# Four inverse-root chains of a decoder step: from log and exp on ScalarE to a square root on ScalarE and a reciprocal on VectorE

## The chip, the cores and the metric

The kernel runs on one core of one Trainium2 chip. The time is the device time of one execution in microseconds, and a kernel's time is the median of its runs. The engines that matter here are TensorE (PE, with its weight loads as PEld), VectorE (DVE), ScalarE (ACT), GpSimd (POOL) and the queue that issues most transfers (SP).

## The reference

One inference step of a two-layer hybrid decoder for a prompt of 256 tokens and eight samples of four new tokens each, 288 tokens in all, width 1024, in fp32. Layer 0 projects to forgetting attention (8 heads of 64) and RWKV-7 time mixing (8 heads of 64), then a dense SwiGLU; layer 1 is a causal pooling mixer, then a mixture of eight experts. Everything that the change touches is an inverse square root:

```
def rms_norm(x, g):
    y = x * lax.rsqrt(jnp.mean(x * x, axis=-1, keepdims=True) + RMS_EPS)
    return y * g

hp = modulate(xp, norm1_g[li], sh1p, sc1p)      # rms_norm, four times: before each mixer and each feed-forward
q, k = rms_norm(heads(q), q_gain), rms_norm(heads(k), k_gain)
kk = kk * lax.rsqrt(jnp.maximum(jnp.sum(kk * kk, axis=-1, keepdims=True), 1e-24))
y = (y - mean) * lax.rsqrt(var + GN_EPS) * ln_w + ln_b                # group norm of the RWKV heads
```

## The kernel before

Activations lie transposed: 128 channels on the partitions, the 288 tokens along the free axis, so that the model's width is 8 such slices. One program is written out by hand for each engine, and the engines meet at counted semaphores; no scheduler reorders anything. On each engine the order is the order of the code. An engine's operation that follows another through memory waits for a semaphore of it, so that nearly every VectorE operation starts after the one before has ended.

TensorE's results go into eight PSUM banks, handed out in turn by `banks.open`: the ninth opening takes the bank of the first, and TensorE waits there until the reader of that bank has given its semaphore. Weights stream from HBM into a ring of six slots of 2 MB.

Seven inverse roots are taken. ScalarE's helper `inverse_root` (L1756) takes a logarithm in place and then an exponential of -0.5 times it. The sums under the roots come from a matmul with ones, which repeats a sum on all partitions that need it, so that the roots are taken on full tiles:

- `root(0)` to `root(3)`, called from the program of ScalarE, on `rstd`, 128 x 288. VectorE's `mean_of(i)` (L1997) writes the mean into `rstd`, waits for `rooted` and multiplies `hT = xT * rstd`; the next matmuls read `hT`.
- the norms of q and k (`qk_rooted`) on the whole `tmpT`, 128 x 2304, in the middle of the input projection. VectorE multiplies them into q and k in its section for `i == 5`, between its copies of the projection's results out of the banks.
- the norm of the RWKV key (`kk_rooted`) on 128 x 1152. VectorE then multiplies `kkT` and after it reads the three banks `bon0` to `bon2`. TensorE opens after `bon2` the banks `kt40`, `kt41`, `ss3`, `kt50`, `kt51`, and the next one, `ss4`, takes the bank of `bon0`. The names `kt` and `ss` are the transposed past keys and the scores of a sample.
- the group norm (`gn_rooted`) on 128 x 1152. After it VectorE finishes the mixer's result `yT` (L2264 to L2270), and the output projection starts.

The compiled program has an ACT_TABLE_LOAD on ScalarE wherever the compiler switches tables: before every `Ln` and every `Exp` of an inverse root, and before none of the copies and squares.

Of the kernel before, what the change touches and what calls it, by code (L numbers as in the profile page):

```python
# [21 lines left out]
ACT = mybir.ActivationFunctionType  # L22
# [7 lines left out]
N = NP + NS  # L30
# [3 lines left out]
HC = HW // P  # L34
# [257 lines left out]
def spread(ap, axis, n):  # L292

    ap = ap.unsqueeze(axis)
    shape = list(ap.shape)
    shape[axis] = n
    return ap.to_broadcast(shape)


def flat(t):  # L300
    return t[:, :, :].rearrange("p a b -> p (a b)")
# [42 lines left out]
def build_program(nc, a, y_p, y_s, k_p, k_s, v_p, v_s, lf_p, lf_s, st_p, st_s, sh_p, sh_s, pool_p, pool_s):  # L344

    ctx = ExitStack()
    with ctx:
        def sb(name, shape, dt=F32):
            return ctx.enter_context(nc.sbuf_tensor(name, shape, dt))

        s = Named(nc, ctx)
        once = Once(s)

        def sums(name, which, n):

            return s(f"sums_{which}"), 3 * ("kks", "bon", "gnm", "gnv").index(name) + n
# [10 lines left out]
        def K(name, rows=P):  # L367
            at, n = CONST[name]
            return const[0:rows, at:at + n]

        ident = K("ident")
        xT = sb("xT", [P, DC, N])
        hT = sb("hT", [P, DC, N])
        tmpT = sb("tmpT", [P, DC, N])
# [5 lines left out]
        rstd = sb("rstd", [P, N])  # L380
# [116 lines left out]
            return t.rearrange("p (c a) k -> p c a k", a=2)[:, :, a, :]  # L497

        small = sb("small", [P, 64])

        plan = sb("plan", [1, NE + 2 * MORE + 1], I32)
        mix_stores = [0]
# [1229 lines left out]
        def _(act):  # L1732
            me = Counted(act)
            chain = s("act_chain")

            def copy(out, in_, sem):
                me.give(act.activation(out, in_, ACT.Copy), sem)  # L1737
# [15 lines left out]
                        act.wait_ge(s("res"), DC * (i - 1) + c + 1)  # L1753
                    me.give(act.activation(tmpT[:, c, :], xT[:, c, :], ACT.Square), s("squared"))

            def inverse_root(v, sem):  # L1756

                me.step(act.activation(v, v, ACT.Ln), chain)
                me.give(act.activation(v, v, ACT.Exp, scale=-0.5), sem)

            def root(i):
                act.wait_ge(s("ms_read"), i + 1)
                inverse_root(rstd[:, :], s("rooted"))

            square_all(0)
            root(0)

            def ada(layer, i):
                k = 12 * layer + i
                act.wait_ge(s("ada_mm"), k + 1)  # L1770
                if k >= 2:
                    act.wait_ge(s("folded"), k - 1)
                copy(adap[layer][:, k % 2, :], banks[f"ada{layer}_{i}"][:, :], s("ada_copied"))
# [4 lines left out]
            def proj_chunk(n):  # L1778
                kind, idx, _, m = WCHUNKS[n]
                dst = {"f": fqkv, "r": rp}[kind]  # L1780
                return dst[0:m, idx, :], banks[f"win{n}"][0:m, 0:N]
# [3 lines left out]
            for i, (_, _, cs) in enumerate(WIN):  # L1785
                for _ in cs:
                    if n % 2:
                        act.wait_ge(s("win_mm"), n + 1)
                        copy(*proj_chunk(n), s("win_act"))
                    n += 1  # L1790
                if i == 2:
                    act.wait_ge(s("win_dve"), HC)
                    act.wait_ge(s("win_act"), HC)
                    me.give(act.activation(flat(tmpT), fqkv[:, 0:2 * HC, :].rearrange("p a b -> p (a b)"), ACT.Square),
                            once.give("qk_squared"))
                ada(0, 4 + i)
                if i == 4:
                    act.wait_ge(s("qkms_read"), 6)
                    inverse_root(flat(tmpT), once.give("qk_rooted"))
            act.wait_ge(*once("lf_abs"))  # L1800
            me.step(act.activation(lftmp[:, 0, :], lftmp[:, 0, :], ACT.Exp), once.give("lf_exp"))
            act.wait_ge(*once("lf_one"))
# [45 lines left out]
            def scores_of(q):  # L1848
                act.wait_ge(s("ss_mm"), q + 1)
                copy(psm[32 * (q % 4):32 * (q % 4) + 32, q // 4, :], banks[f"ss{q}"][0:32, 0:PAST + NT], s("ss_copied"))  # L1850

            for q in range(NB):
                for half in range(2):
                    act.wait_ge(s("kt_mm"), 2 * q + half + 1)
                    if q >= 2:
                        act.wait_ge(s("ss_mm"), q - 1)
                    copy(ktb[:, q % 2, 2 * half:2 * half + 2, 0:PAST],
                         banks[f"kt{q}{half}"][:, :].rearrange("p (c k) -> p c k", c=2), s("kt_copied"))
                copy(ktb[:, q % 2, :, PAST:PAST + NT], fqkv[:, HC:2 * HC, NP + NT * q:NP + NT * (q + 1)], s("kt_copied"))
                if q:  # L1860
                    scores_of(q - 1)
                if q == 2:
                    act.wait_ge(*sums("kks", "read", 3))
                    inverse_root(flat(tmpT)[:, 0:HC * N], once.give("kk_rooted"))
            scores_of(NB - 1)
            act.wait_ge(*once("cum_ready"))
            me.give(act.activation(lw[:, :, NP:N], lw[:, :, NP:N], ACT.Exp), s("decay_exp"))
# [48 lines left out]
            copy(yT[:, HC:2 * HC, NP:N], banks["syt"][:, 0:HC * NS].rearrange("p (c t) -> p c t", c=HC), once.give("syt_copied"))  # L1916
            act.wait_ge(*once("gn_centred"))
            me.give(act.activation(flat(tmpT)[:, 0:HC * N], flat(yT)[:, HC * N:2 * HC * N], ACT.Square), once.give("gn_squared"))
            act.wait_ge(*sums("gnv", "read", 3))
            inverse_root(flat(tmpT)[:, 0:HC * N], once.give("gn_rooted"))  # L1920


            square_all(1)
# [41 lines left out]
        def _(dve):  # L1965
            me = Counted(dve)
            chain = s("dve_chain")
            TT, TS, STT = dve.tensor_tensor, dve.tensor_scalar, dve.scalar_tensor_tensor

            def do(ins, sem=None):  # L1970
                me.step(ins, sem or chain)
# [8 lines left out]
            def mod_tile(layer, i):  # L1980

                dve.wait_ge(s("folded"), 12 * layer + i + 1)
                bias = vT[:, 0, 48 * layer + 4 * i:48 * layer + 4 * i + 4]
                do(TT(modT[layer][:, 4 * i:4 * i + 4, :], banks[f"fold{layer}_{i}"][:, 0:36].rearrange("p (j m) -> p j m", j=4),
                      spread(bias, 2, 9), ALU.add), s("mod_ready"))
# [11 lines left out]
            def mean_of(i):  # L1997
                dve.wait_ge(s("ms_ready"), i + 1)
                do(TS(rstd[:, :], banks[f"ms{i}"][:, 0:N], 1.0 / D, RMS_EPS, ALU.mult, ALU.add), s("ms_read"))
                dve.wait_ge(s("rooted"), i + 1)  # L2000
                do(TT(hT[:, :, :], xT[:, :, :], spread(rstd[:, :], 1, DC), ALU.mult))  # L2001

            def by_seq(ap):
# [32 lines left out]
            for i, (_, _, cs) in enumerate(WIN):  # L2036
                for kind, idx, _, m in cs:
                    if n % 2 == 0:
                        dve.wait_ge(s("win_mm"), n + 1)
                        src = banks[f"win{n}"][0:m, 0:N]  # L2040
                        if kind == "l":
                            do(TS(rstd[0:H, :], src, fbias[:, 0:1], None, ALU.add), s("win_dve"))
                        else:
                            do(dve.tensor_copy({"f": fqkv, "r": rp}[kind][0:m, idx, :], src), s("win_dve"))
                    n += 1
                if i == 2:
                    dve.wait_ge(*once("vec2_turned"))
                    do(dve.tensor_copy(vT[:, 1:3, :], banks["vec2"][:, 0:2 * P].rearrange("p (i f) -> p i f", i=2)),
                       once.give("vec2_copied"))
                    qg = vT[:, 1, VB_QG:VB_QG + 1]  # L2050
                    do(TS(qg, qg, DH ** -0.5, None, ALU.mult))
                if i == 4:

                    for k in range(6):
                        dve.wait_ge(s("qkms"), k + 1)
                        do(TS(flat(tmpT)[:, 384 * k:384 * (k + 1)], banks[f"qkms{k}"][:, 0:384], 1.0 / DH, RMS_EPS, ALU.mult, ALU.add),
                           s("qkms_read"))
                if i == 5:
                    dve.wait_ge(*once("qk_rooted"))
                    dve.wait_ge(s("win_act"), HC)  # L2060
                    for part, g, sem in ((1, VB_KG, "k_ready"), (0, VB_QG, "q_ready")):
                        v = fqkv[:, HC * part:HC * (part + 1), :].rearrange("p a b -> p (a b)")
                        r = flat(tmpT)[:, HC * N * part:HC * N * (part + 1)]
                        do(STT(v, v, vT[:, 1, g:g + 1], r, ALU.mult, ALU.mult), once.give(sem))
                if i:
                    mod_tile(0, 3 + i)
# [52 lines left out]
            def fl(t):  # L2119
                return t.rearrange("p a b -> p (a b)")  # L2120
# [16 lines left out]
                do(TS(flat(tmpT)[:, 384 * i:384 * (i + 1)], banks[f"kks{i}"][:, 0:384], 1e-24, None, ALU.max), s("sums_read"))  # L2137
            dve.wait_ge(*once("kk_rooted"))
            r = flat(tmpT)[:, 0:HC * N]
            do(STT(fl(kkT), fl(kkT), -1.0, r, ALU.mult, ALU.mult))  # L2140

            for i in range(3):
# [118 lines left out]
                   s("sums_read"))  # L2261
            dve.wait_ge(*once("gn_rooted"))
            r = flat(tmpT)[:, 0:HC * N]
            do(TT(y2, y2, r, ALU.mult))  # L2264
            for c in range(HC):
                v = yT[:, HC + c, :]
# [355 lines left out]
```

## Time and profile before

| | |
|---|---|
| median of 3 runs | 1998.54 us (1998.26 to 2000.01) |
| the profiled execution | 2002.73 us, of which the span of the trace is 2000.9 us |
| PE busy | 1812.9 us (91% of the span), 9750 instructions |
| DVE busy | 413.6 us (21%), 772 instructions |
| ACT busy | 225.0 us (11%), 452 instructions |
| POOL busy | 185.2 us (9%), 198 instructions |
| mean granted TensorE clock | 0.917 of full speed |

The shares are averages over stages of different kinds. From about 940 us on the program is the experts, a long run of matmuls; before that, dependent steps of several engines alternate with runs of matmuls. All seven inverse roots lie before 913 us. Times in the rows are microseconds from the start of the span, unless a column says nanoseconds.

### The profile page before, as it was taken

What the parts mean: (1) busy time and instruction counts of PE and PEld (TensorE: products, weight loads), DVE (VectorE), ACT (ScalarE), POOL (GpSimd) and SP (SyncE); (2) the same over time, 40 slices, a digit from 0 to 9 for tenths busy, and PEclk for the clock granted to TensorE, in tenths of its full rate; (3) what the DMA queues carried; (4) which work ended last, traced back from release to release, by engine and by line L of the source; (5) the groups of instructions that cost most, each with busy time, mean ns of one, the idle gap of its engine ahead of it and who ended that gap; (6) DMA issues with size and microseconds to landing.
All of it is one profiled execution on the core that took longest, in us unless ns stands there. A gap on an engine that the chain in (4) does not pass through costs nothing.

```text
span 2000.9 us, 22754 instructions
## 1 busy us (share of the span) xinstructions
PE 1812.9 (91%) x9750; PEld 1166.1 (58%) x9751; DVE 413.6 (21%) x772; ACT 225.0 (11%) x452; POOL 185.2 (9%) x198
## 2 busy tenths in 40 slices
PE   6999687575789999967999999999999999999998
PEld 4766344465467777745555555666555555566664
DVE  2012643857220111174100000001000000010002
ACT  2022142110110000022100000000000000000001
POOL 4002701835000000021000000000000000000000
PEclk8999587656689999977999999999999999999999
DMA  9761031100364554840899999965999999889991
GB/s 346 268 231 64 25 112 31 43 1 4 142 217 158 196 195 167 300 183 11 303 369 339 361 334 347 339 247 199 357 362 364 363 361 367 300 305 383 378 389 64
DMA packets 216499, 476.59 MB, mean 238 GB/s; under 512 B 15823, under 2 KB 24403, under 8 KB 215971
## 3 DMA queue, kind: packets, MB, share of 16 engines
q1 hardware_dynamic: 212971, 471.94, 64.5%
q0 software_dynamic: 3232, 3.08, 0.5%
q8 instruction: 80, 1.31, 0.3%
q14 instruction: 24, 0.20, 0.0%
q10 hardware_dynamic: 192, 0.07, 0.0%
HBM read 470.79 MB, written 4.62 MB: 238 GB/s over the span
## 4 chain that ended last, share of the span: by engine, by line
PE 84%; DVE 5%; POOL 3%; SPq 2%; ACT 2%; DMA 2%; issue 2%; DVEq 0%; POOLq 0%; ACTq 0%
PE bank L1261 82%; POOL ring L2455 2%; DMA ring<-in_ada_w 1%; POOL other L2464 1%; PE bank L749 1%; ACT ring L1737 1%; DVE xT L2017 1%; SPq L2564 1%; SPq L2529 0%; DVE ring L2109 0%; DVE ring L2100 0%; DVE hT L2001 0%; SPq L2555 0%; PE bank L1394 0%; DVE yT L2326 0%
## 5 line engine op out<-in xcount | busy, mean ns | idle before, releaser
L1261 PE MATMUL bank<-other,ring 128*128 128x192 f32 (+4 forms) x3360 | 491.3, 314 | 51.7 <-POOL ring L2455 29.3
L1261 PEld LDWEIGHTS bank<-other,ring 128*128 128x128 f32 (+1 forms) x3360 | 454.2, 193 | 108.9 <-issue 58.8
L1261 PE MATMUL bank<-ring,tmpT 128*64 128x512 f32 (+2 forms) x1120 | 340.1, 604 | 0.0
L1261 PE MATMUL bank<-hT,ring 128*128 128x288 f32 (+2 forms) x1472 | 306.7, 384 | 9.3 <-DVE hT L2013 9.3
L1261 PEld LDWEIGHTS bank<-hT,ring 128*128 128x128 f32 (+2 forms) x1472 | 234.6, 191 | 80.4 <-issue 18.8
L1261 PE MATMUL bank<-ring,other 128*64 128x512 f32 x1120 | 247.8, 595 | 0.6 <-issue 0.6
L1261 PEld LDWEIGHTS bank<-ring,tmpT 128*64 128x64 f32 (+2 forms) x1120 | 106.1, 149 | 204.1 <-issue 202.2
L1261 PEld LDWEIGHTS bank<-ring,other 128*64 128x64 f32 x1120 | 78.2, 137 | 147.7 <-issue 146.6
L1015 DVE TENSOR_TENSOR other<-other,bank 64x512 f32<-64x512 f32 x35 | 23.8, 679 | 641.7 <-ACT other L883 641.7
L1261 PE MATMUL bank<-ring 128*64 128x64 f32 (+6 forms) x468 | 78.9, 413 | 13.5 <-ACT ring L1737 8.8
L1261 PE MATMUL bank<-hT,other 128*128 128x288 f32 (+4 forms) x304 | 69.3, 420 | 6.6 <-DVE hT L993 5.8
L1261 PEld LDWEIGHTS bank<-ring 128*64 128x64 f32 (+4 forms) x468 | 48.0, 204 | 40.3 <-ACT ring L1737 13.4
L2455 POOL TENSOR_TENSOR ring<-ring,const 64x256 f32<-64x256 f32 x48 | 63.7, 1326 | 54.8 <-DVE ring L2217 46.6
L1737 ACT ACTIVATE ring<-bank 128x512 f32<-128x512 f32 (+8 forms) x110 | 44.9, 437 | 175.6 <-PE bank L1261 114.3
L1261 PEld LDWEIGHTS bank<-hT,other 128*128 128x128 f32 (+2 forms) x304 | 46.2, 193 | 29.8 <-issue 19.8
L877 ACT ACTIVATE other<-bank 128x384 f32<-128x384 f32 (+2 forms) x42 | 18.3, 437 | 379.0 <-PE bank L1261 379.0
L1009 DVE TENSOR_TENSOR tmpT<-other,bank 128x384 f32<-128x384 f32 (+2 forms) x42 | 20.5, 488 | 186.7 <-PE bank L1261 144.7
L883 ACT ACTIVATE other<-bank 64x512 f32<-64x512 f32 x35 | 20.8, 593 | 337.6 <-PE bank L1261 337.6
L1261 PE MATMUL bank<-ring,silucT 128*32 128x512 f32 x384 | 46.6, 616 | 4.9 <-DMA ring<-in_ada_w 4.9
L2287 DVE TENSOR_TENSOR other<-other,bank 128x288 f32<-128x288 f32 x22 | 10.0, 454 | 163.5 <-PE bank L1261 163.5
L1737 ACT ACTIVATE other<-bank 128x512 f32<-128x512 f32 (+4 forms) x44 | 22.4, 518 | 177.7 <-PE bank L1261 143.8
L1261 PE MATMUL bank<-yT,other 128*128 128x288 f32 x80 | 26.0, 492 | 16.1 <-DVE yT L2270 10.5
(310 smaller groups left out, 1052.3 us busy)
## 6 DMA issues: line engine op xcount, KB each, us to landing
ring<-in_moe_w_gate SPq DMA_DIRECT2D x56, 2048.0 KB, 10.2
ring<-in_moe_w_up SPq DMA_DIRECT2D x56, 2048.0 KB, 11.1
ring<-in_moe_w_down SPq DMA_DIRECT2D x56, 2048.0 KB, 9.6
ring<-in_ada_w SPq DMA_DIRECT2D x24, 2048.0 KB, 13.7
ring<-in_w_in SPq DMA_DIRECT2D x5, 2048.0 KB, 12.6
ring<-in_ffn_w_gate SPq DMA_DIRECT2D x5, 2048.0 KB, 10.2
ring<-in_ffn_w_up SPq DMA_DIRECT2D x5, 2048.0 KB, 9.1
ring<-in_ffn_w_down SPq DMA_DIRECT2D x5, 2048.0 KB, 17.4
```

The source lines that it names most:

```text
L749: last = pe.transpose(B[TURN][:, HALF * j:HALF * (j + 1)], ea[:, P * j:P * (j + 1)], ident[0:HALF, 0:HALF])
L877: act.activation(sgw[:, 2 * half:2 * half + 2, 0:n], by_half(B[X + half], n), ACT.Silu).then_inc(s("w_silu"), 1)
L883: act.activation(sg, B[GU][HALF:P, :], ACT.Silu).then_inc(s("l_silu"), 1)
L1009: dve.tensor_tensor(actw[:, w % 2, j, 0:n], sgw[:, j, 0:n], by_half(B[X + half], n), ALU.mult).then_inc(s("w_act"), 1)
L1015: dve.tensor_tensor(ea, sg, B[GU][0:HALF, :], ALU.mult).then_inc(s("l_act"), 1)
L1261: return pe.matmul(out, lhsT, rhs, start=start, stop=stop, skip_group_check=True)
L1737: me.give(act.activation(out, in_, ACT.Copy), sem)
L2017: do(STT(xT[:, j, 0:NP], src[:, 0:NP], gate_[:, j, 0:1], xT[:, j, 0:NP], ALU.mult, ALU.add))
L2287: do(TT(ffact[:, i % 2, n % 4, :], ffsilu[:, n % 2, :], banks[f"up{n}"][:, 0:N], ALU.mult), s("act_ready"))
L2455: me.step(pool.tensor_tensor(nm[o, n % 2], of(gt[o, n % 2], a_)[:, :, 0:L], mask, ALU.mult), s("nm_ready") if a_ else s("pool_chain"))
L2464: me.step(pool.tensor_tensor(vk, spread(sval[:, t, :], 2, DH), spread(svec[:, t, 3, :], 1, 32), ALU.mult), s("vk_ready"))
L2564: sp.dma_start(svec[2 * H * q + f:2 * H * (q + 1):2].rearrange("p t i k -> p (t i) k"), scratch[q].rearrange("t i h k -> h (t i) k")).then ...
```

## The change

The seven uses of `inverse_root` become `root_of`, one square root on ScalarE, and VectorE takes a reciprocal in place right after its wait for the root. `root(i)` and the group norm get `early_root`, a square root of one element into an unused cell, ahead of the wait. The norms of q and k and of the RWKV key get no early root.

```
+        root_of_one = small[0:1, 61:62]
...
-            def inverse_root(v, sem):
-                me.step(act.activation(v, v, ACT.Ln), chain)
-                me.give(act.activation(v, v, ACT.Exp, scale=-0.5), sem)
+            def early_root():
+                act.activation(root_of_one, K("ident")[0:1, 0:1], ACT.Sqrt)
+            def root_of(v, sem):
+                me.give(act.activation(v, v, ACT.Sqrt), sem)
             def root(i):
+                early_root()
                 act.wait_ge(s("ms_read"), i + 1)
-                inverse_root(rstd[:, :], s("rooted"))
+                root_of(rstd[:, :], s("rooted"))
...
-                    inverse_root(flat(tmpT), once.give("qk_rooted"))
+                    root_of(flat(tmpT), once.give("qk_rooted"))
...
-                    inverse_root(flat(tmpT)[:, 0:HC * N], once.give("kk_rooted"))
+                    root_of(flat(tmpT)[:, 0:HC * N], once.give("kk_rooted"))
...
+            early_root()
             act.wait_ge(*sums("gnv", "read", 3))
-            inverse_root(flat(tmpT)[:, 0:HC * N], once.give("gn_rooted"))
+            root_of(flat(tmpT)[:, 0:HC * N], once.give("gn_rooted"))
...
                 dve.wait_ge(s("rooted"), i + 1)
+                do(dve.reciprocal(rstd[:, :], rstd[:, :]))
                 do(TT(hT[:, :, :], xT[:, :, :], spread(rstd[:, :], 1, DC), ALU.mult))
...
                     dve.wait_ge(*once("qk_rooted"))
+                    do(dve.reciprocal(flat(tmpT), flat(tmpT)))
...
             dve.wait_ge(*once("kk_rooted"))
             r = flat(tmpT)[:, 0:HC * N]
+            do(dve.reciprocal(r, r))
             do(STT(fl(kkT), fl(kkT), -1.0, r, ALU.mult, ALU.mult))
...
             dve.wait_ge(*once("gn_rooted"))
             r = flat(tmpT)[:, 0:HC * N]
+            do(dve.reciprocal(r, r))
             do(TT(y2, y2, r, ALU.mult))
```

On ScalarE the compiled program has 20 table loads before and 13 after. At the group norm and `root(1)`, ScalarE's order before:

```order
L1918 ACTIVATE tmpT<-yT 128x1152 [waits vector_once]
L1758 ACT_TABLE_LOAD
L1758 ACTIVATE tmpT<-tmpT 128x1152 [waits sums_read]
L1759 ACT_TABLE_LOAD
L1759 ACTIVATE tmpT<-tmpT 128x1152 [waits act_chain]
L1754 ACTIVATE tmpT<-xT 128x288 [waits res] x8
L1758 ACT_TABLE_LOAD
L1758 ACTIVATE rstd<-rstd 128x288 [waits ms_read]
L1759 ACT_TABLE_LOAD
```

and the same place of the changed kernel:

```order
L1922 ACTIVATE tmpT<-yT 128x1152 [waits vector_once]
L1759 ACT_TABLE_LOAD
L1759 ACTIVATE small<-const 1x1
L1762 ACTIVATE tmpT<-tmpT 128x1152 [waits sums_read]
L1755 ACTIVATE tmpT<-xT 128x288 [waits res] x8
L1759 ACTIVATE small<-const 1x1
L1762 ACTIVATE rstd<-rstd 128x288 [waits ms_read]
```

In both, a load stands ahead of the waiting activation and carries no wait itself. The load and the second activation behind the wait are gone.

Later than the RWKV key's root ScalarE takes exponentials of the cumulated decay. Its order there before (`ss_mm` rows are the copies of the scores, `vector_once` is VectorE's `cum_ready` and then `psm_shifted`):

```order
L1737 ACTIVATE ring<-bank 32x260 [waits ss_mm] x2
L1867 ACTIVATE other<-other 128x4x32 [waits vector_once]
L1868 ACTIVATE tmpT<-tmpT 128x1024
L1869 ACTIVATE tmpT<-tmpT 128x1024
L1870 ACTIVATE hT<-hT 128x1024
```

and after:

```order
L1738 ACTIVATE ring<-bank 32x260 [waits ss_mm] x2
L1871 ACT_TABLE_LOAD
L1871 ACTIVATE other<-other 128x4x32 [waits vector_once]
L1872 ACTIVATE tmpT<-tmpT 128x1024
L1873 ACTIVATE tmpT<-tmpT 128x1024
L1874 ACTIVATE hT<-hT 128x1024
```

A table load has come in behind the copies. The same holds, not shown, for the first exponential of the forget gate (L1801) and for that of the router (L1955).

VectorE's order at the RWKV key, before:

```order
L2137 TENSOR_SCALAR tmpT<-bank 128x384 [waits sums_mm,sums_read] x2
L2140 SCALAR_TENSOR_TENSOR yT<-yT,tmpT 128x1152 [waits scalar_once,sums_read]
L2145 TENSOR_TENSOR other<-bank,other 128x384 [waits sums_mm,dve_chain]
L2145 TENSOR_TENSOR other<-bank,other 128x384 [waits sums_mm,sums_read] x2
L2147 TENSOR_SCALAR other<-other 128x1152 [waits sums_read]
```

and after:

```order
L2144 TENSOR_SCALAR tmpT<-bank 128x384 [waits sums_mm,sums_read] x2
L2147 RECIPROCAL tmpT<-tmpT 128x1152 [waits scalar_once,sums_read]
L2148 SCALAR_TENSOR_TENSOR yT<-yT,tmpT 128x1152 [waits dve_chain]
L2153 TENSOR_TENSOR other<-bank,other 128x384 [waits sums_mm,dve_chain]
L2153 TENSOR_TENSOR other<-bank,other 128x384 [waits sums_mm,sums_read] x2
L2155 TENSOR_SCALAR other<-other 128x1152 [waits sums_read]
```

The reciprocal has come in between the wait for ScalarE (`scalar_once`) and the multiplication; the reads of the `bon` banks stand behind both. The other six reciprocals stand at the same kind of place.

## Rows read from the trace of the kernel before

**Rows 1.** The page's chain that ended last: shares of the span by engine.
```profile
PE 84%; DVE 5%; POOL 3%; SPq 2%; ACT 2%; DMA 2%; issue 2%; DVEq 0%; POOLq 0%; ACTq 0%
```

**Rows 2.** ScalarE's groups by form: busy us, mean ns | idle before.
```profile
L1758 ACT ACT_TABLE_LOAD x7 | 9.0, 1283 | 0.1
L1759 ACT ACT_TABLE_LOAD x7 | 9.0, 1283 | 0.1
```

**Rows 3.** VectorE's groups by form, same columns.
```profile
L2001 DVE TENSOR_TENSOR hT<-xT,rstd 128x2304 f32<-128x2304 f32 x4 | 10.2, 2559 | 9.3 <-ACT rstd L1759 9.3
...
L2264 DVE TENSOR_TENSOR yT<-yT,tmpT 128x1152 f32<-128x1152 f32 x1 | 1.4, 1359 | 3.8 <-ACT tmpT L1759 3.8
...
L2108 DVE RECIPROCAL small<-small 128x2 f32<-128x2 f32 x8 | 1.3, 166 | 0.3
...
L2362 DVE RECIPROCAL other<-other 128x3 f32<-128x3 f32 x1 | 0.2, 178 | 0.0
...
L2363 DVE TENSOR_TENSOR other<-other 128x3 f32<-128x3 f32 x1 | 0.2, 166 | 0.0
```

**Rows 4.** Timeline at root(1): start, us, engine, line, operation [idle before].
```profile
570.94 0.46 DVE L1999 TENSOR_SCALAR rstd<-bank 128x288 f32<-128x288 f32 x1 [2.95 <-PE bank L1261]
571.43 0.44 ACT L1758 ACTIVATE rstd<-rstd 128x288 f32<-128x288 f32 x1 [1.66 <-DVE rstd L1999]
571.89 1.28 ACT L1759 ACT_TABLE_LOAD   x1
...
573.73 2.56 DVE L2001 TENSOR_TENSOR hT<-xT,rstd 128x2304 f32<-128x2304 f32 x1 [2.33 <-ACT rstd L1759]
```

**Rows 5.** Timeline at the group norm, to the output projection.
```profile
522.88 1.16 ACT L1758 ACTIVATE tmpT<-tmpT 128x1152 f32<-128x1152 f32 x1 [3.27 <-DVE tmpT L2260]
524.06 1.28 ACT L1759 ACT_TABLE_LOAD   x1
...
526.62 1.36 DVE L2264 TENSOR_TENSOR yT<-yT,tmpT 128x1152 f32<-128x1152 f32 x1 [3.77 <-ACT tmpT L1759]
...
532.68 14.87 PE L1261 MATMUL bank<-yT,other 128*128 128x288 f32 x48 [10.51 <-DVE yT L2270]
```

**Rows 6.** Timeline in the input projection, around VectorE's multiplications of q and k.
```profile
147.06 0.46 DVE L2044 COPY other<-bank 128x288 f32<-128x288 f32 x1 [7.30 <-PE bank L1261]
147.56 2.87 DVE L2064 SCALAR_TENSOR_TENSOR other<-other,vT,tmpT 128x1152 f32<-128x1152 f32 x2
...
167.90 0.51 PE L1261 MATMUL bank<-hT,ring 128*128 128x288 f32 x1
```

**Rows 7.** Timelines of ScalarE, VectorE and TensorE at the RWKV key.
```profile
286.51 1.16 ACT L1758 ACTIVATE tmpT<-tmpT 128x1152 f32<-128x1152 f32 x1
...
290.26 1.36 DVE L2140 SCALAR_TENSOR_TENSOR yT<-yT,tmpT 128x1152 f32<-128x1152 f32 x1 [16.11 <-ACT tmpT L1759]
...
291.65 1.74 DVE L2145 TENSOR_TENSOR other<-bank,other 128x384 f32<-128x384 f32 x3
...
296.07 1.94 PE L1261 MATMUL bank<-ring 128*32 128x260 f32 x8
...
299.84 1.09 PE L1447 MATMUL bank<-const,ring 128*128 128x128 f32 x8 [0.79 <-DMA ring<-in_cache_fox_logf]
```

**Rows 8.** Timeline at the exponentials of the decay.
```profile
311.30 0.31 ACT L1867 ACTIVATE other<-other 128x128 f32<-128x128 f32 x1
...
315.08 0.69 DVE L2158 TENSOR_REDUCE small<-ring 128x2 f32<-128x520 f32 x1 [2.07 <-ACT ring L1872]
```

**Rows 9.** Timeline of VectorE behind root(0), and at the forget gate and router.
```profile
40.74 0.20 DVE L1984 TENSOR_TENSOR modT<-bank,vT 128x36 f32<-128x36 f32 x1 [9.60 <-PE bank L1261]
...
186.28 0.44 ACT L1801 ACTIVATE ring<-ring 8x288 f32<-8x288 f32 x1 [2.83 <-DVE ring L2075]
...
930.83 0.17 DVE L2369 COPY small<-bank 128x8 f32<-128x8 f32 x1 [2.15 <-PE bank L1261]
```

**Rows 10.** Stretch of the windows view: us, PE busy, granted clock, DMA share, GB/s.
```profile
532.60:535.00 2.40, 2.32 (x5) 0.50 0.24 59
```

## The prediction

> **What bounds the kernel now.** I read the chain that ended last first, then the groups by form of ScalarE and VectorE, then the timelines at the seven roots. The chain is 84% TensorE; VectorE has 5% of it and ScalarE 2% [rows 1]. So nearly nothing of this change touches the bound by its busy time; what counts is where TensorE stands still because a root is not there yet. At root(1) the reader sees such a place: VectorE writes the mean, ScalarE takes the logarithm, loads a table for 1.28 us and takes the exponential, and VectorE sat idle 2.33 us before it multiplies [rows 4]. The four such waits sum to 9.3 us [rows 3]. The group norm is the same with longer tiles: VectorE waits 3.77 us, and TensorE starts the output projection right after VectorE's last step, after 10.51 us of idleness [rows 5]. The table loads are 14 of 1283 ns [rows 2], but the seven ahead of a logarithm are not on the path: at the group norm ScalarE sat idle 3.27 us between its load and the logarithm [rows 5]. Transfers have 2% of the chain [rows 1], and those of weights in it lie ahead of 45 us; nothing behind these places is there to take up a delay, so a microsecond at one of them is a microsecond of the kernel.
>
> **What is removed.** Per root, behind the wait, one table load and one activation. For root(1) to root(3) the square root should last what the logarithm does, 0.44 us, and would end where the load now starts; the removed part is 1.28 + 0.44 = 1.72 us and small gaps [rows 4]. At the group norm it is 1.28 + 1.16 = 2.44 us [rows 5]. The early root of one element and its load run in ScalarE's idle time, where the load of the logarithm ran: cost nothing while the 3.27 us (and 1.66 us at root(1)) of idleness behind it cover the 0.2 us that a short activation takes [rows 4, 5]. Without that cover it would be 0.2 us each.
>
> **What is added: the reciprocal.** Its price at 288, 1152 and 2304 elements decides everything, and the trace has it only for 2 and 3 elements. An ordinary two-operand pass costs 1359 ns for 1152 elements and 2559 ns for 2304, so 1.04 ns for each further element and about 160 ns for one element [rows 3]. The reciprocal of 2 elements takes 166 ns: its second element costs 6 ns. That of 3 takes 178 ns, in a tile where an ordinary pass over 3 elements takes 166 ns, so about 164 ns for one, and the two others cost 7 ns each. Taking the two reciprocals against one another, the third element costs 12 ns [rows 3]. The lower bound is the ordinary 1.04 ns, the upper one 12 ns. These are differences of single clock steps and of different tiles, but none of the readings that use a reciprocal lies near 1 ns. I take 7 ns, from the comparison within one tile: 153 + 7N ns, that is 2.17 us for 288, 8.22 us for 1152, 16.28 us for 2304.
>
> The Trainium skill speaks against the change here: "VectorE: DVE Perf Modes", section "Walkthrough: the 8-slice pipeline in each mode", says that a reciprocal runs iterative divide operations with a repeat count of 8. Read as 8 cycles of that page's 0.96 GHz clock for each element, an estimate of 8.33 ns, it would make the sum below about 16 us in place of 9.5.
>
> **The sum, place by place.**
> - root(0): VectorE next waits, 9.60 us long, for the modulation at 40.74 us [rows 9]. The reciprocal's 2.2 us against 1.7 us saved vanish there: 0. With less cover it would be +0.4.
> - norms of q and k: ScalarE is long done when VectorE comes to them. The reciprocal goes in after the copy that ends at 147.52 us, ends at 163.8, and the two multiplications (2.87 us) at 166.7, the next read of a bank (0.20 us, the same operation as in [rows 9]) at 167.0. Late next is TensorE's opening at 167.90, the ninth after the bank that this read frees [rows 6]. 0.9 us are left: 0. Beyond 7.4 ns an element TensorE would stand there, 2.3 us for each further ns.
> - RWKV key: the square root ends at 286.51 + 1.16 = 287.67 us. The reciprocal runs from 287.77 to 295.99, the multiplication (1.36) to 297.4, and the first read of a `bon` bank (a third of 1.74) to 298.0 [rows 7]. TensorE wants that bank for `ss4` at 296.07: it waits 1.95 us. Of these 0.79 us would have been idle before the next transposes at 299.84 [rows 7]: +1.2. At 6.0 ns an element this term ends.
> - decay exponentials: before, ScalarE starts them at 311.30 at once behind the last copy, the table of exponentials being loaded. Now the load stands there. VectorE waits for the end of this run with 2.07 us of idleness, so all of the load is on the path: +1.28, by the 1283 ns of the other loads [rows 2, 8].
> - group norm: the square root ends at 522.88 + 1.16 = 524.04, the reciprocal at 524.14 + 8.22 = 532.36, and VectorE multiplies at 532.4 where it was 526.62: +5.8 [rows 5].
> - root(1) to root(3): square root to 571.87, reciprocal from 571.97 to 574.14, multiplication at 574.17, before 573.73: +0.44, three times +1.3 [rows 4].
> - forget gate: the new load falls in 2.83 us of idleness ahead of that exponential; 0. Router: the load delays VectorE's six small steps by about 1.3 us, but VectorE waits 2.15 us for TensorE behind them; 0 [rows 9]. Without that cover each would cost 1.28.
>
> Together 0 + 0 + 1.2 + 1.28 + 5.8 + 1.3 = **9.6 us slower**. Against its own profiled execution of 2002.73 us that is 2012.3; that one is 4.2 us above the median of the runs, 1998.54, and the difference is put on the median: **2008.1 us**.
>
> A second rule of the skill concerns the loads. Rows first: at root(1) the load starts at 571.89; 1.28 us of load and 0.44 us of exponential end at 573.61, and VectorE multiplies at 573.73 [rows 4]. "ScalarE: Activation LUTs", section "What ACT_TABLE_LOAD costs", adds a drain of about 1.38 us to each. By it the load added at the decay would cost 2.66 us and the sum be 1.4 us larger; there is no room for a drain in these rows, and I stay with 1.28.
>
> **The rivals.**
> - *The reciprocal is an ordinary pass* at 1.04 ns an element: 0.46, 1.36 us. For it speaks only that all other passes here are; against it the 12 ns between the two sizes. Then root(1) to root(3) gain 1.27 us each, the group norm 1.1 us, the key nothing, and the load still costs 1.28: -3.6 us, **1994.9**. This is the case on the other side. It turns at about 2.9 ns an element, where the gains of the four waits just pay the load; if two elements went per cycle it would be 1.2 us lower still.
> - *Between*, 3 to 5 ns an element, if the small reciprocals carry a fixed part that I have put on the elements: at 4.5 ns the group norm is +2.9, the three roots -0.8, the load +1.28: **2001.9**.
> - *The steep reading*, 12 ns: 3.6, 14.0 and 27.8 us. The projection then loses 10.5, the key 6.9, the group norm 11.5, the three roots 5.6, the load 1.28: +35.8, **2034**. For it speaks the pair of reciprocals; against it that they lie in different tiles, with strides of their own.
> - *TensorE's clock*: after the group norm's 10.51 us of idleness the granted clock is 0.50 of full, 1.2 of 2.4 GHz [rows 5, 10]. A longer wait can't lower it there. The new wait at `ss4` could cost a fall where there was none, some microseconds more; I give it no case of its own but it lies in the range.
>
> **How the numbers follow.** 6 to 9 ns an element has a chance of 0.70 and gives 2005 to 2018, worked as above at 6 and at 9; the ordinary pass 0.12, the cases between 0.08, the steep one 0.10. I leave out the ordinary pass and most of the steep side: 2001 to 2019. A measurement of this kernel tells about 0.2%, 4 us, from no change, its runs lying 1.8 us apart. The ordinary pass at -3.6 is just within it, faster by more only with two elements per cycle: faster 0.05. Within 0.2%: the rest of that case and most of the cases between, 0.14. Slower 0.81.
>
> **What would show it.** The reciprocals' durations at 288, 1152 and 2304 elements, on which all hangs: 2.2, 8.2 and 16.3 us. VectorE's idleness before the reciprocals at 0.6 us for root(1) to root(3) and about 1.3 us at the group norm; the output projection 5.8 us further from the group norm's sums than before. TensorE waiting for a bank at `ss4`, about 2 us, and not at all in the input projection. A load of 1.28 us between the last score copy and the decay's first exponential. Thirteen table loads. I am wrong if the reciprocals take about 1.4 us at 1152 elements (then all stalls shrink), if TensorE stands in the projection, or if the clock falls at `ss4`.

## The result and the profile after

| | before | after |
|---|---|---|
| median of 6 runs each, us | 1999.23 (1997.69 to 2000.6) | 2006.2 (2005.28 to 2008.2) |
| ratio, 95% interval | | 1.0037 (1.0024 to 1.0049) |
| profiled execution, us (span) | 2002.73 (2000.9) | 2007.59 (2005.7) |
| granted clock, mean | 0.917 | 0.92 |

The changed kernel is 7.0 us slower by the medians (4.8 to 9.8 by the interval); 9.6 us were forecast. The page of the profile of the changed kernel, called after from here on, says:

```profile
span 2005.7 us, 22753 instructions
PE 1811.2 (90%) x9750; PEld 1164.4 (58%) x9751; DVE 451.1 (22%) x779; ACT 210.6 (11%) x443; POOL 185.5 (9%) x198
PE 83%; DVE 6%; POOL 3%; SPq 2%; issue 2%; ACT 2%; DMA 1%; ACTq 0%; DVEq 0%; POOLq 0%
```

TensorE still holds the chain [rows 1]; VectorE has gone from 5% to 6% of it. The prediction hung on the reciprocal's price. VectorE's groups by form, after (busy us, mean ns | idle before):

```profile
L2066 DVE RECIPROCAL tmpT<-tmpT 128x2304 f32<-128x2304 f32 x1 | 14.6, 14553 | 0.0
L2006 DVE RECIPROCAL rstd<-rstd 128x288 f32<-128x288 f32 x4 | 7.8, 1953 | 2.3 <-ACT rstd L1762 2.3
L2272 DVE RECIPROCAL tmpT<-tmpT 128x1152 f32<-128x1152 f32 x1 | 7.4, 7353 | 1.3 <-ACT tmpT L1762 1.3
```

From 1152 to 2304 elements it takes 14553 - 7353 = 7200 ns more, 6.25 ns an element; from 288 to 1152, 5400 ns, 6.25 again. The constant is 7353 - 1152 x 6.25 = 153 ns, the very one of the forecast, and 153 + 2 x 6.25 = 166 ns is the small reciprocal of [rows 3]. The idle time before the four of 288 elements is 2.3 us, against 9.3 before the multiplications of [rows 3]: the waits for ScalarE shrank as meant, and VectorE's own work took their place.

Timeline of after at root(1) and at the group norm (start, us, engine, line, operation, idle before), which answer to [rows 4] and [rows 5]:

```profile
576.56 0.46 DVE L2004 TENSOR_SCALAR rstd<-bank 128x288 f32<-128x288 f32 x1 [2.95 <-PE bank L1262]
577.05 0.44 ACT L1762 ACTIVATE rstd<-rstd 128x288 f32<-128x288 f32 x1 [2.87 <-DVE rstd L2004]
577.59 1.95 DVE L2006 RECIPROCAL rstd<-rstd 128x288 f32<-128x288 f32 x1 [0.58 <-ACT rstd L1762]
579.58 2.56 DVE L2007 TENSOR_TENSOR hT<-xT,rstd 128x2304 f32<-128x2304 f32 x1
```

```profile
524.36 1.16 ACT L1762 ACTIVATE tmpT<-tmpT 128x1152 f32<-128x1152 f32 x1 [2.98 <-DVE tmpT L2268]
525.62 7.35 DVE L2272 RECIPROCAL tmpT<-tmpT 128x1152 f32<-128x1152 f32 x1 [1.30 <-ACT tmpT L1762]
533.01 1.36 DVE L2273 TENSOR_TENSOR yT<-yT,tmpT 128x1152 f32<-128x1152 f32 x1
...
539.07 6.10 PE L1262 MATMUL bank<-yT,other 128*128 128x288 f32 x15 [15.41 <-DVE yT L2279]
```

From the mean (VectorE's 0.46 us) to the multiplication are 3.02 us at root(1), 2.79 before: +0.23. At the group norm, from the square root's start to the multiplication 8.65 us, before 3.74: +4.91, and TensorE stands 15.41 us where it stood 10.51.

ScalarE at the decay exponentials, after, answers to [rows 8]:

```profile
311.33 0.38 ACT L1738 ACTIVATE ring<-bank 32x260 f32<-32x260 f32 x1 [2.52 <-PE bank L1262]
311.72 1.28 ACT L1871 ACT_TABLE_LOAD   x1
313.02 0.31 ACT L1871 ACTIVATE other<-other 128x128 f32<-128x128 f32 x1
...
316.79 0.69 DVE L2166 TENSOR_REDUCE small<-ring 128x2 f32<-128x520 f32 x1 [3.35 <-ACT ring L1876]
```

The new load stands behind the last copy, and VectorE's wait is 3.35 us where it was 2.07: 1.28 us more, the whole load. The first exponential follows 0.02 us behind the load's end. "ScalarE: Activation LUTs" of the Trainium skill, section "What ACT_TABLE_LOAD costs", adds about 1.38 us of drain to each load; these rows have no place for it.

TensorE and VectorE at the RWKV key and `ss4`, after, answer to [rows 7]:

```profile
288.13 7.35 DVE L2147 RECIPROCAL tmpT<-tmpT 128x1152 f32<-128x1152 f32 x1 [15.61 <-ACT tmpT L1762]
...
297.61 1.91 PE L1262 MATMUL bank<-ring 128*32 128x260 f32 x8 [1.62 <-DVE other L2153]
...
300.49 1.09 PE L1448 MATMUL bank<-const,ring 128*128 128x128 f32 x8
```

The forecast wait at `ss4` is there, 1.62 us long, and the transposes behind it at 300.49 wait for nothing, where they had stood 0.79 us for a transfer.

In the input projection (answering to [rows 6]) nothing waits:

```profile
145.91 14.55 DVE L2066 RECIPROCAL tmpT<-tmpT 128x2304 f32<-128x2304 f32 x1
...
163.41 0.20 DVE L1989 TENSOR_TENSOR modT<-bank,vT 128x36 f32<-128x36 f32 x1
...
166.25 10.07 PE L1262 MATMUL bank<-hT,ring 128*128 128x288 f32 x39
```

The read that frees the bank ends at 163.61, and TensorE opens there at 166.25 without a wait. The place is free because of these 2.64 us of cover. ScalarE has thirteen table loads in place of twenty.

### The profile page after: what moved, and what is told of

Read it like the earlier page. It is cut to its first block, busy times and chain, and to the rows that moved or that the text cites. A ratio compares the mean times of both kernels' runs of the same rounds, so it can differ in the third digit from the quotient of the medians.

```text
span 2005.7 us, 22753 instructions
## 1 busy us (share of the span) xinstructions
PE 1811.2 (90%) x9750; PEld 1164.4 (58%) x9751; DVE 451.1 (22%) x779; ACT 210.6 (11%) x443; POOL 185.5 (9%) x198
## 4 chain that ended last, share of the span: by engine, by line
PE 83%; DVE 6%; POOL 3%; SPq 2%; issue 2%; ACT 2%; DMA 1%; ACTq 0%; DVEq 0%; POOLq 0%
PE bank L1262 81%; POOL ring L2464 2%; POOL other L2473 1%; SPq L2538 1%; PE bank L750 1%; SPq L2548 1%; ACT ring L1738 1%; DVE xT L2023 1%; DMA ring<-in_w_in 1%; SPq L2573 1%; DVE ring L2116 0%; DVE ring L2107 0%; DVE hT L2007 0%; DVE tmpT L2272 0%; DVE tmpT L2147 0%
## 6 DMA issues: line engine op xcount, KB each, us to landing
ring<-in_ada_w SPq DMA_DIRECT2D x24, 2048.0 KB, 13.5
```

## The experiments

e4 and e8 start from the kernel before, the others from the changed one. Whole times of one and the same kernel spread by 8 to 9 us between runs (before beside e1 to e4: 1998.8, 1994.68 to 2002.55 in 19 runs; beside e5 to e8: 2000.81, 1994.45 to 2003.73 in 12), so most verdicts are read from the place in the trace that the edit touches. Each kernel has one trace, of one execution. `inverse_root` below is the function of before.

**e1: the table of exponentials loaded early at the decay.**

```diff
                     root_of(flat(tmpT)[:, 0:HC * N], once.give("kk_rooted"))
+                    act.preload_act_table(ACT.Exp)
```

> The changed kernel, with the table of exponentials loaded right behind the RWKV key's square root, where ScalarE has idle time, instead of behind the last score copy. Theory (the load is on the path there): the decay's exponentials start at once behind the copy, 1.28 us earlier, and the time falls by about 1.3 us, to 1.0030 of before (some 2005). Rival (VectorE's own steps end last there): no change, 1.0037.

Measured: 2005.18 us (2004.71 to 2007.23, 5 runs), ratio 1.0035 (1.0021 to 1.0048). ScalarE and VectorE of e1:

```profile
286.42 1.28 ACT L1869 ACT_TABLE_LOAD   x1
...
313.91 0.70 DVE L2167 TENSOR_REDUCE small<-ring 128x2 f32<-128x520 f32 x1 [2.07 <-ACT ring L1877]
```

The load lies in the scores, and VectorE's wait is 2.07 us again, as before the change. So the load's 1.28 us were on the path and this line takes them back; the whole time, 1.0 us below after, agrees but could not have shown it. From the key's squares on ScalarE to that reduction e1 needs 45.28 us and before 45.08. With the load gone, 0.20 us are left for the key's reciprocal; e6 below shows how little that says.

**e2: the group norm with logarithm and exponential again.**

```diff
-            early_root()
             act.wait_ge(*sums("gnv", "read", 3))
-            root_of(flat(tmpT)[:, 0:HC * N], once.give("gn_rooted"))
+            inverse_root(flat(tmpT)[:, 0:HC * N], once.give("gn_rooted"))
...
-            do(dve.reciprocal(r, r))
```

> The changed kernel with the group norm alone taken back to log and exp, no reciprocal there. Theory (7.35 us of reciprocal against 2.44 us of load and exponential, all of it on the path): 4.9 us faster than the changed kernel, 1.0012 of before (some 2001.5). Rival (the change's cost sits in its loads and in TensorE's clock, the reciprocal being partly made up for later): less than half of that, 1.0025 or more.

Measured: 2003.79 us (1998.74 to 2007.27, 10 runs), ratio 1.0025 (1.0014 to 1.0035). The rows of e2:

```profile
520.89 1.16 ACT L1762 ACTIVATE tmpT<-tmpT 128x1152 f32<-128x1152 f32 x1 [3.66 <-DVE tmpT L2271]
...
524.63 1.36 DVE L2275 TENSOR_TENSOR yT<-yT,tmpT 128x1152 f32<-128x1152 f32 x1 [3.77 <-ACT tmpT L1763]
...
530.70 14.07 PE L1262 MATMUL bank<-yT,other 128*128 128x288 f32 x48 [10.50 <-DVE yT L2281]
```

Activation to multiplication is 3.74 us, as in [rows 5], and TensorE's idle time is 10.50 us: the place gives back 4.91 us. The whole time did not come down by as much: 2.4 us by the medians, short of the 4.9 us expected, and from its ratio of 1.0025 alone the rival could not be told apart. The ten runs are 8.5 us apart. The trace settles more: from the group norm's squares to VectorE's mean at root(1), with the output projection in between, e2 takes 53.38 us, after 57.86 and e1 58.23. (Before, which runs e2's steps there, takes 53.79.) So the 4.5 to 4.9 us are still saved at root(1), and up to there the reciprocal is not made up for. Why the median of the whole times shows only half of it stays open; the last section has a candidate. e3 pulls the same lever harder.

**e3: the group norm's reciprocal three times** (the second undoes the first, so the values stand).

```diff
             do(dve.reciprocal(r, r))
+            do(dve.reciprocal(r, r))
+            do(dve.reciprocal(r, r))
```

> The changed kernel with three reciprocals in a row at the group norm in place of one (two of them undo one another). Theory: twice 7.35 us and 0.04 us of gap each on the path, 14.8 us slower than the changed kernel, 1.0111 of before (some 2021). Rival (part of a stall there is given back, TensorE's clock returning earlier behind it): 1.0105 or less, 12 to 13.5 us; with the clock unmoved the runs of matmuls behind it last the same.

Measured: 2022.37 us (2020.2 to 2026.42, 4 runs), ratio 1.0125 (1.011 to 1.0141), 16.2 us above after. The rows of e3:

```profile
522.44 7.35 DVE L2272 RECIPROCAL tmpT<-tmpT 128x1152 f32<-128x1152 f32 x1 [1.30 <-ACT tmpT L1762]
...
537.21 7.35 DVE L2274 RECIPROCAL tmpT<-tmpT 128x1152 f32<-128x1152 f32 x1
544.60 1.36 DVE L2275 TENSOR_TENSOR yT<-yT,tmpT 128x1152 f32<-128x1152 f32 x1
```

From the square root's start to the multiplication are 23.43 us, for 8.65 in after: 14.78 us more, two reciprocals with their gaps. TensorE stands 30.19 us before the output projection, 14.78 more than in after, and from the squares to the mean at root(1) e3 takes 73.45 us, 15.6 more. So the trace shows nothing given back up to root(1), against the rival's 12 to 13.5 us. The 16.2 us of the whole time agree, but the intervals of the two ratios are too wide to exclude the rival by themselves.

**e4: logarithm and exponential from one table set, loaded ahead of the waits.** It starts from before. At root(0), the key and root(2) the set that has both functions is loaded by name.

```diff
             def root(i):
+                if i in (0, 2):
+                    act.preload_act_table_set("natural_log_exp_and_others")
...
+                    act.preload_act_table_set("natural_log_exp_and_others")
                     act.wait_ge(*sums("kks", "read", 3))
```

> The kernel before, with log and exp everywhere, but the one table set that serves both loaded ahead of the waits of root(0), the RWKV key and root(2). Theory (a load between log and exp costs its 1.28 us where the wait is on the path): gone from the forget gate, the group norm and root(1) to root(3), five times 1.28, while tanh needs a load of its own that comes onto the path, so 5 us faster than before, 0.9974 (some 1994). Rival (the set's own tables cost more, or TensorE's clock takes the gain back): 0.9985 to 1.000.

Measured: 1992.96 us (1991.22 to 1998.1, 10 runs), ratio 0.9974 (0.9965 to 0.9984): faster than both kernels, and the 0.9974 that was expected. The rows of e4 at the group norm, and VectorE's at root(1):

```profile
519.34 1.16 ACT L1758 ACTIVATE tmpT<-tmpT 128x1152 f32<-128x1152 f32 x1 [4.50 <-DVE tmpT L2263]
520.54 1.16 ACT L1759 ACTIVATE tmpT<-tmpT 128x1152 f32<-128x1152 f32 x1
521.80 1.36 DVE L2267 TENSOR_TENSOR yT<-yT,tmpT 128x1152 f32<-128x1152 f32 x1 [2.49 <-ACT tmpT L1759]
...
566.55 2.56 DVE L2004 TENSOR_TENSOR hT<-xT,rstd 128x2304 f32<-128x2304 f32 x1 [1.05 <-ACT rstd L1759]
```

At the group norm no load stands between the two activations. VectorE waits 2.49 us in place of 3.77, and 1.05 in place of 2.33: 1.28 us at each of these places and also at root(2) and root(3), and nothing is handed to VectorE. At the forget gate VectorE's step that waits for the second function starts 2.80 us after the gains are taken, in place of 4.07, so 1.27 us earlier. The groups of this trace have 8 loads, before had 20. "ScalarE: Activation LUTs" of the Trainium skill, section "Table sets: the hidden batching unit", says that a logarithm and then an exponential need one load, as a joint set has both. Here that holds in e4, where the set is asked for by name, and not in before, where each activation got a load of its own [rows 2].

One load moved onto the path instead, the one ahead of the tanh, which before had found its table in place. Timeline of e4:

```profile
256.05 0.28 ACT L1737 ACTIVATE yT<-bank 128x128 f32<-128x128 f32 x1 [1.24 <-PE bank L1261]
256.34 1.28 ACT L1837 ACT_TABLE_LOAD   x1
257.64 0.44 ACT L1837 ACTIVATE other<-other 64x288 f32<-64x288 f32 x1
```

TensorE waits 2.14 us there in place of 0.71, so this costs 1.43 us. The local gains are then 4 x 1.28 + 1.27 - 1.43 = 5.0 us, and the ratio says 5.2.

**e5: two more reciprocals of 1152 elements at q and k** (again they undo each other), added to after; one run.

```diff
                     do(dve.reciprocal(flat(tmpT), flat(tmpT)))
+                    do(dve.reciprocal(flat(tmpT)[:, 0:HC * N], flat(tmpT)[:, 0:HC * N]))
+                    do(dve.reciprocal(flat(tmpT)[:, 0:HC * N], flat(tmpT)[:, 0:HC * N]))
```

> The changed kernel with two more reciprocals of 1152 elements (they undo one another) behind the one of q and k. In the changed kernel VectorE's next reads of banks end 2.6 us before TensorE wants the first of them. Theory (nine openings of cover): TensorE waits 14.8 - 2.6 = 12 us there, and the forget gate's steps come 12 us later after their start. Rival (no cover, or cover of more banks): 14.8 us, or under 8.

Measured: 2019.84 us, 13.6 above after's median. VectorE and TensorE of e5:

```profile
169.55 7.35 DVE L2068 RECIPROCAL tmpT<-tmpT 128x1152 f32<-128x1152 f32 x1
...
179.84 0.20 DVE L1989 TENSOR_TENSOR modT<-bank,vT 128x36 f32<-128x36 f32 x1
...
180.19 13.99 PE L1262 MATMUL bank<-hT,ring 128*128 128x288 f32 x48 [12.21 <-DVE modT L1989]
```

TensorE stands 12.21 us, as the theory had it (12), and the row names VectorE's read of a modulation bank, the chain of steps that the forecast gave. Of 14.77 us added, 2.56 were covered, close to the 2.64 read off after's rows. The place was free by its slack, not because VectorE is out of TensorE's way.

**e6: the key with logarithm and exponential again**; one run.

```diff
-                    root_of(flat(tmpT)[:, 0:HC * N], once.give("kk_rooted"))
+                    inverse_root(flat(tmpT)[:, 0:HC * N], once.give("kk_rooted"))
...
-            do(dve.reciprocal(r, r))
```

> The changed kernel with the RWKV key's norm alone taken back to log and exp. Theory: TensorE's wait of 1.6 us for a bank there goes, worth some tenths because transfers of pages end there as well, and the decay's load goes, 1.28 us, since the key's exponential leaves its table: 1.4 to 1.9 us from the square of the key to VectorE's sum over the sample scores. Rival (the load moves elsewhere onto the path): less than 0.6 us.

Measured: 2002.9 us. From the key's squares to the reduction are 44.75 us. Against e2 and e3 (46.5 us), which run after's steps there, that is 1.8 us less, within the 1.4 to 1.9 expected. Against e1 (45.28), which like e6 has no load on the path, it is 0.5 us less, where e1 beside before gave 0.2. But before and e6 run the same instructions on this stretch and are themselves 0.33 us apart, so the key's reciprocal is shown to cost some tenths at most, and its size is not told closer. `ss4` waits for no bank here; TensorE stands 0.24 and 0.62 us for transfers instead, the second of them here:

```profile
303.86 1.09 PE L1448 MATMUL bank<-const,ring 128*128 128x128 f32 x8 [0.62 <-DMA ring<-in_cache_fox_logf]
```

**e7: root(0) to root(3) with logarithm and exponential again**; one run.

```diff
-                early_root()
                 act.wait_ge(s("ms_read"), i + 1)
-                root_of(rstd[:, :], s("rooted"))
+                inverse_root(rstd[:, :], s("rooted"))
...
-                do(dve.reciprocal(rstd[:, :], rstd[:, :]))
```

> The changed kernel with root(0) to root(3) alone taken back to log and exp. Theory: from VectorE's mean to its multiplication 2.79 us as in the kernel before, instead of 3.02, so 0.23 us less at each of root(1) to root(3), 0.7 us in all; the time by itself can't tell that. If TensorE's phase of clock makes the 1.2 us by which the router's matmuls came later in the changed kernel, it can stand here or not, whatever the router's load; if the load makes it, it stays only where a load stands there, and here none does, since root(3) leaves the table of exponentials.

Measured: 2008.24 us, too near to after for one run to say more. In the trace of e7 at root(1):

```profile
577.01 0.46 DVE L2007 TENSOR_SCALAR rstd<-bank 128x288 f32<-128x288 f32 x1 [2.95 <-PE bank L1262]
...
579.80 2.56 DVE L2009 TENSOR_TENSOR hT<-xT,rstd 128x2304 f32<-128x2304 f32 x1 [2.33 <-ACT rstd L1763]
```

That is 2.79 us, as before: the 0.23 us of each of the three are the square root and reciprocal in place of load and exponential, and nothing else. From the mean of root(1) to the multiplication of root(3) after takes 341.81 us, e7 341.24 and before 341.61; the 0.7 us that three times 0.23 make can't be told closer than that. What e7 says of the router stands with the router below.

**e8: e4 with the tanh's table loaded among the score exponentials.**

```diff
                 if k < 7:
                     exponentials(k + 1)
+                if k == 6:
+                    act.preload_act_table_set("sigmoid_and_others")
```

> The kernel before with the one table set for log and exp, as tried already, and the sigmoid's set, which has tanh too, loaded behind the last exponential of the prompt's attention, so that neither tanh nor sigmoid finds a load ahead of it. Theory: tanh starts 1.28 us earlier behind its wait, of which some is paid back by ScalarE's copies in the attention, 0.5 to 1.3 us faster than that kernel, 0.9970 of before (some 1993). Rival (the copies behind the load are just as much on the path): 0.9974, the same.

Measured: 1989.49 us (1985.04 to 1995.4, 7 runs), ratio 0.9946 (0.9926 to 0.9965), the fastest version here. Timeline of e8:

```profile
249.63 1.28 ACT L1828 ACT_TABLE_LOAD   x1
...
254.97 0.28 ACT L1737 ACTIVATE yT<-bank 128x128 f32<-128x128 f32 x1 [1.24 <-PE bank L1261]
255.14 0.43 ACT L1839 ACTIVATE other<-other 64x288 f32<-64x288 f32 x1
```

The tanh starts 0.17 us after the copy's start, in e4 1.59 us after it: 1.42 us nearer. That is what the edit is shown to do. From that copy to the key's squares e8 takes 13.18 us and e4 13.95, so of the 1.42 us only 0.8 are left there in these two traces. The step from e4's 0.9974 to 0.9946 is 0.0028, or 5.6 us by the ratios and 3.5 us by the medians, and the intervals meet at 0.9965. Both were measured beside different runs of before, and 0.9970 was expected. The part beyond 1.4 us is not accounted for, and that e8 is faster than e4 is likely but not shown by the times alone.

## Why the prediction was nearly right

Slower was forecast and is what came, by the mechanism that the sum gave. What differs is one number, the 7 ns an element, which is 6.25. It came from the reciprocal of 3 elements, whose 178 ns [rows 3] lie 6 ns above the 153 + 3 x 6.25 = 172 ns of the line; the other reading of the same rows, 6 ns for the second element, was the nearer one. "VectorE: DVE Perf Modes" of the Trainium skill, section "Walkthrough: the 8-slice pipeline in each mode", speaks of a repeat count of 8; read as 8 cycles an element it was the estimate of 8.33 ns, and the rows show less.

| place | forecast, us | measured, us | read from |
|---|---|---|---|
| root(0) | 0 | 0 | VectorE waits 5.70 and 6.91 us for TensorE behind it |
| forget gate | 0 | 0 | VectorE's steps 4.08 for 4.07 |
| norms of q and k | 0 | 0 | no wait; e5: 2.6 us of cover |
| RWKV key | +1.2 | +0.2 to +0.5 | e1 with before, e1 with e6; before and e6, alike there, differ by 0.3 |
| decay exponentials | +1.28 | +1.28 | wait 3.35 for 2.07; e1 |
| group norm | +5.8 | +4.9 | 8.65 for 3.74; e2, e3 |
| root(1) to root(3) | 3 x 0.44 | 3 x 0.23 | 3.02 for 2.79; e7 |
| router | 0 | 0 | see below |
| sum | 9.6 | 7.1 to 7.4 | whole times: 7.0 |

That the sum and the whole times meet within 0.4 us is partly luck: the interval of the ratio, 4.8 to 9.8 us, holds the forecast's 9.6 as well as the 7.1 to 7.4, and only the rows decide between them.

**The mis-sized term is the reciprocal's price**: 8.22 us at 1152 elements was 7.35, and 2.17 at 288 was 1.95. The 0.9 us at the group norm and 0.2 at each of three roots are this alone.

**The key** was forecast at +1.2 us, from a wait of 1.95 less 0.79 of transfer waits. With 7.35 us, the same steps give 287.77 + 7.35 = 295.12, the multiplication to 296.5, the first bank read to 297.1, and a wait of 1.0 us at `ss4`; e1 has 1.17 and e3 0.97. The transfer waits that it swallows are 0.79 and, two steps on, 0.15 us, so 0.94. What is left is 0.1 to 0.2, in keeping with the few tenths measured. By these rows a slightly dearer reciprocal would have counted in full, and a cheaper one not at all. The wait is 1.33 us in e2 and 1.62 in e7 and after; the last two are those in which the clock had fallen just ahead (below).

**The rivals.** The ordinary pass (1.36 us at 1152 elements) and the steep reading (14 us) are both excluded by 7.35 us, and the case between at 4.5 ns by the same row. (The further gain at two elements per cycle is 1.05 us by the forecast's own terms, 0.52 ns on 3 x 288 + 1152 elements, and not 1.2.) The fall of the clock at `ss4` did not come: the granted clock stays at 1.00 from 290 to 310 us in after, e1, e2, e3, e6 and e7.

**The router.** There after is 1.2 us later than before between root(3)'s multiplication and the rank copy (19.46 us for 18.28), where the forecast had 0 for the load. The five other traces that have the load there stand thus: e1, e2, e5 and e6 need 19.5 us, e3 17.89. The three others without it need 17.9 (e4 and e8) and 18.1 us (e7). e7's expectation named this: the 1.2 us would be gone there if the load made them, and they are, so e7 does not clear the load. e3 does, by its rows beside those of after. VectorE's rank copies are

```profile
937.83 0.17 DVE L2378 COPY small<-bank 128x8 f32<-128x8 f32 x1 [2.06 <-PE bank L1262]
```

in after and

```profile
948.37 0.17 DVE L2380 COPY small<-bank 128x8 f32<-128x8 f32 x1 [0.51 <-PE bank L1262]
```

in e3. Counted from root(3)'s multiplication, the load starts at 14.5 us in both and VectorE's last small step behind it at 17.2 us in both. What differs is TensorE: in the 3 us from the load's start on, its granted clock is 1.00 in e3 and 0.50 in after, so that at the load's start it had come back in the one and not in the other. The load comes too late to have kept it from coming back. The load itself has 0.5 us of cover in e3 and 2.1 in after. The windows of after, in front of the rank copy and behind it (us, PE busy (x), PEld, DVE, ACT and POOL busy (x), granted clock, DMA share, GB/s):

```profile
930.00:936.00 6.00, 6.00 (x35) 5.47 (x34) 3.46 (x23) 4.27 (x8) 0.00 (x0) 0.50 0.00 0
946.00:950.00 4.00, 4.00 (x15) 2.77 (x15) 0.49 (x1) 0.44 (x1) 0.00 (x0) 0.96 0.00 0
```

and the same places of before:

```profile
927.00:931.00 4.00, 3.73 (x32) 3.46 (x30) 1.60 (x9) 2.31 (x6) 0.00 (x0) 0.90 0.00 0
939.00:943.00 4.00, 4.00 (x11) 2.62 (x11) 0.49 (x1) 0.44 (x1) 0.00 (x0) 0.69 0.00 0
```

In after the granted clock is at 0.50 (1.2 of 2.4 GHz) ahead of the ranks and back at 0.96 in the gather; in before it is the other way about. From root(3)'s multiplication to the end of the span the six traces with the load take 1087.4 to 1087.9 us and the four without it 1087.9 to 1088.4: what is lost ahead of the ranks comes back behind them, and the load costs nothing there, as forecast. Why five of the six traces with the load have the late return of the clock and none of the four without it stays open.

## What to carry to other kernels

Price a replacement by the size of its tile and not by its count: a reciprocal at 6.25 ns an element on a VectorE that TensorE waits for beats a table load of 1.28 us and an activation only in small tiles. An estimate of the break-even from root(1)'s and the group norm's rows (+0.23 us at 288 elements, +4.91 at 1152, so 5.4 ns an element) is near 250 elements. When a table load is on the path, ask first whether one set holds both functions and load it by name ahead of the wait; that gave the 1.28 us back at each wait and put nothing elsewhere, as long as the next function with another table (here the tanh) gets its load in idle time too. Before believing a whole time, look at the place: the 0.23 us at each root repeats to 0.01 us in the traces, where whole times differed by 8. But a longer stretch of one trace carries the clock's own differences, and two kernels that are alike on it show how large they are.

## What the runs showed that was not expected

**The same program, another clock.** TensorE's granted clock does not change at the same instruction in each execution. After and e1 run the same program up to the key. Windows of TensorE alone in after, over the transposes and scores at 278 to 286 us (us, PE busy, granted clock, DMA share, GB/s):

```profile
278.00:282.00 4.00, 2.53 (x12) 0.84 0.83 240
282.00:286.00 4.00, 4.00 (x19) 0.74 0.87 253
```

and of e1:

```profile
278.00:282.00 4.00, 2.47 (x15) 1.00 0.88 254
282.00:286.00 4.00, 3.60 (x22) 1.00 0.81 248
```

Eight matmuls of the scores took 3.50 us at the fallen clock in after and 1.94 in e1. TensorE had stood for a transfer just before in both, 3.19 us in after and 2.81 in e1. e7 fell too and had stood 3.29 us; before, e2, e3 and e6, with 2.71 to 2.87 us, did not. So from the key's squares to the reduction after needed 48.61 us, e2 and e3, the same program there without that fall, 46.5: 2.1 us that are the clock's and not the reciprocal's. Another such place is where the clock comes back behind 320 us. All engines' windows of after (columns as at the router):

```profile
328.00:330.00 2.00, 2.00 (x9) 0.40 (x12) 0.00 (x0) 0.00 (x0) 0.00 (x0) 0.50 0.00 0
```

and of e2:

```profile
328.00:330.00 2.00, 2.00 (x21) 0.78 (x13) 0.31 (x1) 0.00 (x0) 0.00 (x0) 1.00 0.00 0
```

From VectorE's reduction to the group norm's squares all seven of before, after, e1, e2, e3, e6 and e7 run the same steps; before, after, e1 and e7 take 201.4 to 202.1 us, e2, e3 and e6 198.3 to 199.0. So one stretch alone moves a span by 3 us or more, whatever the change. It may be behind e2's miss and part of e8's excess, but no run here held the clock fixed and each kernel has only one trace, so that stays argued.

**GpSimd beside a reciprocal.** A copy of 128x64 on GpSimd took 0.24 us inside the key's reciprocal; in before such a copy took 0.24 us with VectorE idle and 1.19 beside its two-input multiplication. The key's reciprocal did not hold that copy up; these are three single rows, on an engine whose spans are rough.
